# Differential attention: the joining factor moves to GpSimd, reciprocals go ahead of a maximum, row sums of squares go to ScalarE

## What is computed

```
def block(args):
    qb, start = args
    q_chunk = (start + jnp.arange(Q_BLOCK)) // CHUNK
    mask = key_chunk[None, :] <= q_chunk[:, None]
    s = jnp.einsum('bqhcd,bkhcd->bhcqk', qb, k).astype(jnp.float32)
    p = jax.nn.softmax(jnp.where(mask, s, -jnp.inf), axis=-1)
    a = p[:, :, 0] - lam * p[:, :, 1]
    return jnp.einsum('bhqk,bkhe->bqhe', a.astype(v.dtype), v)
...
o = rms_norm_2(o, subln_g) * (1.0 - lam_init)
return o.reshape(B, S, H * DIFF_V_DIM) @ w_out
```

## Time and profile before

| what | value |
|---|---|
| median of three runs | 2334.5 us |
| the profiled execution | 2334.52 us |
| its span | 2332.8 us |
| TensorE busy | 2311.1 us, 99% of the span |
| VectorE busy | 791.1 us, 34% |
| ScalarE busy | 853.1 us, 37% |
| GpSimd busy | 1173.1 us, 50% |
| PE busy from 1231 to 1322 us (the 32 tiles) | 82.63 us of 91 |
| granted TensorE clock | 1.00 |

### The profile page before, as it was taken

The page is one execution under the profiler, slowest core; times in us unless marked ns, Lnnn a source line. Parts: engine busy times, 40 slices in busy tenths (PEclk is TensorE's granted clock), DMA queues, the critical chain, the costliest instruction groups (busy, mean ns, idle before and its releaser), DMA issues.

```text
span 2332.8 us, 26900 instructions
## 1 busy us (share of the span) xinstructions
PE 2311.1 (99%) x11100; PEld 1882.2 (81%) x11100; DVE 791.1 (34%) x1372; ACT 853.1 (37%) x1258; POOL 1173.1 (50%) x978
## 2 busy tenths in 40 slices
PE   9999999999999999999999999999999999999999
PEld 7888888888977888888887688888887757888887
DVE  3222204864223222201467652022046954210310
ACT  4322214514343332222446543123156464421330
POOL 6544445636654544444552365444446944544442
PEclk9999999999999999999999999999999999999999
DMA  4323223212332232322220133233231202323322
GB/s 153 106 90 99 99 90 111 91 56 90 127 109 73 93 106 90 100 99 90 91 91 19 55 93 106 90 96 103 90 96 63 91 1 73 91 93 106 91 90 90
DMA packets 147584, 209.61 MB, mean 90 GB/s; under 512 B 7259, under 2 KB 113926, under 8 KB 147462
## 3 DMA queue, kind: packets, MB, share of 16 engines
q1 hardware_dynamic: 147462, 207.89, 27.6%
HBM read 205.77 MB, written 2.10 MB: 89 GB/s over the span
## 4 chain that ended last, share of the span: by engine, by line
PE 91%; DVE 4%; POOL 3%; issue 1%; ACT 1%; DMA 0%; SPq 0%; DVEq 0%; POOLq 0%; ACTq 0%
PE ps L1547 28%; PE ps L1548 28%; PE ps L1549 28%; POOL wlo L801 1%; DVE small L2967 1%; PE ps L2385 1%; PE ps L1919 1%; PE ps L1941 1%; PE ps L2310 0%; PE ps L2356 0%; PE ps L2366 0%; PE ps L2026 0%; DMA xrows<-in_x 0%; DVE small L2975 0%; DVE d_a L2980 0%
## 5 line engine op out<-in xcount | busy, mean ns | idle before, releaser
L801 POOL TENSOR_TENSOR wlo<-raw,whi 128x512 fp32r<-128x512 f32 x772 | 1006.1, 1336 | 973.2 <-ACT whi L1026 951.3
L1026 ACT ACTIVATE whi<-raw 128x2048 fp32r<-128x2048 f32 x184 | 350.6, 1905 | 632.5 <-DMA raw<-in_mlp_w 302.1
L1547 PE MATMUL ps<-hh,whi 128*128 128x512 f32 x1432 | 561.6, 392 | 0.0
L1549 PE MATMUL ps<-hh,wlo 128*128 128x512 f32 x1432 | 557.4, 389 | 0.0
L1548 PE MATMUL ps<-hl,whi 128*128 128x512 f32 x1432 | 557.3, 389 | 0.0
L1547 PEld LDWEIGHTS ps<-hh,whi 128*128 128x128 f32 x1432 | 268.8, 188 | 58.2 <-issue 2.3
L1549 PEld LDWEIGHTS ps<-hh,wlo 128*128 128x128 f32 x1432 | 268.8, 188 | 56.2
L1548 PEld LDWEIGHTS ps<-hl,whi 128*128 128x128 f32 x1432 | 268.9, 188 | 56.0 <-issue 1.2
L1547 PE MATMUL ps<-gh,whi 128*128 128x512 f32 x736 | 286.3, 389 | 0.0
L1548 PE MATMUL ps<-gl,whi 128*128 128x512 f32 x736 | 286.3, 389 | 0.0
L1549 PE MATMUL ps<-gh,wlo 128*128 128x512 f32 x736 | 286.3, 389 | 0.0
(11 more groups left out here) (472 smaller groups left out, 2869.4 us busy)
## 6 DMA issues: line engine op xcount, KB each, us to landing
raw<-in_mlp_w SPq DMA_DIRECT2D x64, 1024.0 KB, 5.4
raw<-in_ffn_w_up SPq DMA_DIRECT2D x22, 1024.0 KB, 5.2
raw<-in_ffn_w_down SPq DMA_DIRECT2D x22, 1024.0 KB, 4.8
raw<-in_ffn_w_gate SPq DMA_DIRECT2D x21, 1024.0 KB, 5.1
raw<-in_w_in SPq DMA_DIRECT2D x12, 1024.0 KB, 5.2
raw<-in_diff_w_in SPq DMA_DIRECT2D x12, 1024.0 KB, 5.0
raw<-in_xattn_w_kv SPq DMA_DIRECT2D x8, 1024.0 KB, 5.0
raw<-in_dsa_w_in SPq DMA_DIRECT2D x8, 1024.0 KB, 4.9
```

The source lines that it names most:

```text
L801: nc.gpsimd.tensor_tensor(wlo[i][:, c], raw[i][:, c], whi[i][:, c].bitcast(F32), ALU.subtract).then_inc(s_lo, 1)
L1026: nc.scalar.activation(whi[i][:, 0:width(made[0])], raw[i][:, 0:width(made[0])], ACT.Copy)\
L1547: nc.tensor.matmul(dst, w_hi, x_hi, start=start, stop=False)
L1549: return nc.tensor.matmul(dst, w_lo, x_hi, start=False, stop=stop)
```

## The change

1. VectorE's `weights` is cut in two. `inverse_sums(u)` takes the reciprocals; for qt = 0 it also makes the joining factor, as before, now in another cell. For qt = 1 to 3 the factor is made on GpSimd by `weight_factor(u)` from the same numbers. `weights(u)` waits for it and makes `d_a`.
2. The order on VectorE changes. At qt = 1 and 2 the reciprocals of tile u+1 go ahead of `max_(u+2)`, at qt = 0 and 3 behind it. `weights(u+1)` is always the last of the step, so behind `max_(u+2)` and, at qt = 0, behind `low` and `rows_copy`.
3. `row_sums` is gone. ScalarE squares each head in four instructions of 128x128 that also give the row sums, in place of one of 128x512, and GpSimd makes the half variance (`head_variance`).
4. On GpSimd the order is now by tile. Block b+12 is split a quarter at a time in steps 6 to 9, block b+13 in steps 28 to 31, and block b+14 behind the last head.
5. Two semaphores are merged into one with other counts, with no change of order.

```
+            def split_piece(q):
+                b = cut[0]
+                i = b % NBUF
+                if q == 0:
+                    pool.wait_ge(s_hi, b)
+                nc.gpsimd.tensor_tensor(wlo[i][:, ts(q, 512)], raw[i][:, ts(q, 512)],
+                                        whi[i][:, ts(q, 512)].bitcast(F32), ALU.subtract).then_inc(s_lo, 1)
+                if q == 3:
+                    cut[0] += 1
...
             def diff(b):
                 split_to(b + DIFF_BLOCKS - 1)
-                for h in range(8):
-                    head_scaled(h)
-                    if h in (0, 5, 6):
-                        split_to(b + DIFF_BLOCKS + (0, 5, 6).index(h))
+                for u in range(32):
+                    h, qt = divmod(u, 4)
+                    if qt:
+                        weight_factor(u)
+                    if qt == 2 and h:
+                        head_variance(h - 1)
+                    if qt == 3 and h:
+                        head_scaled(h - 1)
+                    if 6 <= u < 10 or 28 <= u:
+                        split_piece(u % 4 if u >= 28 else u - 6)
+                head_variance(7)
+                head_scaled(7)
+                split_to(b + DIFF_BLOCKS + 2)
+
+            def weight_factor(u):
+                h, qt = divmod(u, 4)
+                k, r = 12 + 2 * slot(u), 32 + 8 * (h % 2) + 2 * qt
+                n = 3 * h + qt
+                pool.wait_ge(s_drec, n)
+                if n > 1:
+                    pool.wait_ge(s_da, u if qt > 1 else u - 1)
+                nc.gpsimd.tensor_scalar(small[:, 8:9], small[:, k:k + 1], small[:, r + 1:r + 2], lam[:, 2:3],
+                                        ALU.mult, ALU.mult).then_inc(s_dfac, 1)
+
+            def head_variance(h):
+                pool.wait_ge(s_dosq, h + 1)
+                nc.gpsimd.tensor_scalar(newton[:, 0, 0:4], small[:, 24:28], -0.5 / P, -0.5 * EPS, ALU.mult, ALU.add)\
+                    .then_inc(s_dovar, 1)
...
                     act.wait_ge(s_dor, h + 1)
                     if h:
-                        act.wait_ge(s_doss, h)
-                    nc.scalar.activation(d_osq[:, :], d_o[:, h % 2, :], ACT.Square).then_inc(s_dosq, 1)
+                        act.wait_ge(s_dovar, h)
+                    for st in range(ST):
+                        r = nc.scalar.activation(d_osq[:, ts(st, P)], d_o[:, h % 2, ts(st, P)], ACT.Square,
+                                                 accum_out=small[:, 24 + st:25 + st])
+                    r.then_inc(s_dosq, 1)
...
                 for u in range(32):
                     h, qt = divmod(u, 4)
-                    if qt == 2:
-                        weights(u + 1)
+                    if qt in (1, 2):
+                        inverse_sums(u + 1)
                     if u < 30:
                         max_(u + 2)
-                    if qt != 2 and u < 31:
-                        weights(u + 1)
+                    if qt in (0, 3) and u < 31:
+                        inverse_sums(u + 1)
                     if qt == 0 and h >= 2:
                         low(h - 2)
                     if qt == 0 and h:
                         rows_copy(h - 1)
-                    if qt == 1 and h:
-                        row_sums(h - 1)
+                    if u < 31:
+                        weights(u + 1)
```

More of the change, by code:

```diff
@@ L456, in two_blocks @@
         s_fsq = sem("s_fsq")
-        s_frow = sem("s_frow")
+        s_drec = sem("s_drec")
+        s_dfac = sem("s_dfac")
         s_fcopy = sem("s_fcopy")
@@ L463, in two_blocks @@
         s_dosq = sem("s_dosq")
-        s_doss = sem("s_doss")
         s_dors = sem("s_dors")
@@ L2084, in diff @@
                                                     ident[:, :])
-                        r.then_inc(s_frow, 1)
+                        r.then_inc(s_fsq, 1)
                     half_group(b + 2 * g + 1, 4 * g, 1, (0, 1))
@@ L2263, in dsa @@
                         if j == 1 and a == 1:
-                            pe.wait_ge(s_fsq, 9)
+                            pe.wait_ge(s_fsq, 10)
                             pe.wait_ge(s_x, x0 + 8)
@@ L2950, in diff @@
                     if g == 0:
-                        dve.wait_ge(s_frow, 1)
+                        dve.wait_ge(s_fsq, 6)
                         V.tensor_copy(rstd[:, :], ps[:, 6, :]).then_inc(s_fcopy, 1)
@@ L2967, in max_, with inverse_sums @@
                     V.tensor_reduce(small[:, k:k + 2], two, AX_X, ALU.min).then_inc(s_dmax, 1)
-                def weights(u):
+                def inverse_sums(u):
                     h, qt = divmod(u, 4)
@@ L2973, in weights @@
                     k, r = 12 + 2 * slot(u), 32 + 8 * (h % 2) + 2 * qt
-                    dv.link(V.reciprocal(small[:, r:r + 2], small[:, k:k + 2]))
-                    dv.link(V.tensor_scalar(small[:, 8:9], small[:, k:k + 1], small[:, r + 1:r + 2],
+                    rec = V.reciprocal(small[:, r:r + 2], small[:, k:k + 2])
+                    if qt:
+                        rec.then_inc(s_drec, 1)
+                        return
+                    dv.link(rec)
+                    dv.link(V.tensor_scalar(small[:, 9:10], small[:, k:k + 1], small[:, r + 1:r + 2],
                                             lam[:, 2:3], ALU.mult, ALU.mult))
+                def weights(u):
+                    h, qt = divmod(u, 4)
+                    if qt:
+                        dve.wait_ge(s_dfac, 3 * h + qt)
                     if u >= 3:
@@ L2979, in weights @@
                     nk = P * (qt + 1)
-                    V.scalar_tensor_tensor(out=d_a[:, u % 3, 0:nk], in0=d_p[:, u % 3, 1, 0:nk], scalar=small[:, 8:9],
-                                           in1=d_p[:, u % 3, 0, 0:nk], op0=ALU.mult, op1=ALU.add).then_inc(s_da, 1)
+                    f = 8 if qt else 9
+                    V.scalar_tensor_tensor(out=d_a[:, u % 3, 0:nk], in0=d_p[:, u % 3, 1, 0:nk],
+                                           scalar=small[:, f:f + 1], in1=d_p[:, u % 3, 0, 0:nk],
+                                           op0=ALU.mult, op1=ALU.add).then_inc(s_da, 1)
                 def rows_copy(h):
@@ L2991, in rows_copy @@
                         .then_inc(s_dor, 1)
[L2993 to L3000, removed]
                 def low(h):
@@ L3009, in diff @@
                 max_(1)
+                inverse_sums(0)
                 weights(0)
@@ L3029, in diff @@
                 rows_copy(7)
-                row_sums(7)
                 low(6)
@@ L3043, in dsa @@
                     if t > 5:
-                        dve.wait_ge(s_fsq, t)
+                        dve.wait_ge(s_fsq, t + 1)
                     first = c_esq[:, 0, :] if t == 5 else sq[:, 1, :]
@@ L3047, in dsa @@
                 dve.wait_ge(s_eacc, acc_at(E_DSA) + 3)
-                dve.wait_ge(s_fsq, 8)
+                dve.wait_ge(s_fsq, 9)
                 V.tensor_tensor(sq[:, 0, :], sq[:, 0, :], sq[:, 1, :], ALU.add).then_inc(s_fsq, 1)
```

## The result

The changed kernel takes 2345.31 us in the median of 6 runs (2343.99 to 2346.16), the kernel before 2335.61 us in the same set (6 runs, 2334.26 to 2337.02). The ratio is 1.0042, with an interval of 1.0032 to 1.0052. I had forecast 2340.9 us with a range of 2336.5 to 2343: slower is right, but the time lies above the range. The profiled executions are 2334.52 and 2343.99 us, with spans of 2332.8 and 2341.8, so 9.0 us have to be found in the trace. (The other 0.5 us between these two times lies outside the spans.)

The account below looks back on a forecast made before the run. PE was taken to bound the kernel, with 91% of the chain of waits. To 2334.5 us the forecast added 2.0 for the 32 tiles and 4.4 for the late split: 2340.9 us, range 2336.5 to 2343.

Parts of the forecast that it names:

- The late split: GpSimd splits block b+14 only behind head 7's scaling, so PE stands before that block: +4.4 us, range 4.2 to 5.1.
- The lock-out rule: VectorE with two SBUF inputs and GpSimd reading SBUF exclude each other for a whole instruction; b+14 stall then 4.7 us.
- Nothing later gives it back: Behind PE's wait for block b+14, later work follows PE's own progress, so the 4.4 us delay is not recovered.
- The quarters of blocks b+12 and b+13 come earlier than `use` needs them: On GpSimd, the splits of these two blocks are early enough for their user; no time was added for them.
- The squares: Four ScalarE squares of 1.44 us delay the exponents of qt = 3: +0.35 us a head in heads 2 to 5.
- the sign of being right: Period of a middle head of 11.3 to 11.5 us, named in advance as showing the forecast right.
- Heads 6 and 7: Head 6 was given +0.3 us, an estimate by the same loop; head 7, with no maximum following, 0.
- rival B: The heads gain and lose nothing and only the late split is seen: 2338.9 us, chance 20%.
- Rival A: VectorE's relief reaches PE, whose idle 8.4 us in the 32 tiles could all go: 2330.5 us, chance 6%.
- Rival D: Each tile pays for making the factor on GpSimd, up to 1.26 us per factor: 2347.3 us, chance 5%.
- the sign that I had named for it: VectorE idle waiting for GpSimd's factor, named in advance as showing Rival D.
- Rival C: The late split is hidden by something unseen and only the heads count: 2336.5 us, chance 7%.

Follow-up runs that it names:

- experiment 1: The changed kernel with the split of block b+14 moved ahead of head 7's variance and scaling on GpSimd; 2337.83 us, ratio 1.0013 to the kernel before.
- experiment 5: The kernel before with one edit: the split of block b+14 behind head 7's scaling instead of ahead of it; 2342.17 us, ratio 1.0030.
- Experiment 4: The changed kernel with 19 unneeded matmuls on PE ahead of its wait for block b+14; 2343.46 us, ratio 1.0037 to the kernel before.
- Experiment 2: The changed kernel with the quarters of block b+12 split in steps 7 to 10 instead of 6 to 9; 2342.61 us, ratio 1.0036 to the kernel before.
- experiment 6: Experiment 3 with one 128x512 square on ScalarE, row sums and half variance back on VectorE; 2332.97 us, ratio 0.9991 to the kernel before.
- experiment 7: Experiment 6 with the joining factors back on VectorE, straight ahead of `d_a`; 2335.88 us, ratio 1.0003 to the kernel before.
- experiment 3: The changed kernel with both moves, b+14's split ahead of head 7's scaling and b+12's quarters one step later; 2335.95 us, ratio 1.0005 to the kernel before.
- experiment 8: Experiment 3 with the joining factors back on VectorE, straight ahead of `d_a`; 2336.55 us, ratio 1.0008 to the kernel before.

## Why the prediction was right, and where it failed

*The late split: right.* +4.4 forecast, +4.46 measured; experiment 1 takes it out, experiment 5 makes it alone. The split took 5.38 us, between the undisturbed 5.04 and the 6.00 beside VectorE: its start at 1338.34 overlaps the last `final_scaled`, which ends at 1338.92. Only its first quarter is slow, 1.72 us where the others take 1.25, and it ends at 1340.06. The lock-out rule of the Trainium skill (SBUF — State Buffer, Who interferes with whom), which the prediction put beside its sum, would have it wait for the end of `final_scaled` and end at 1340.17 (1338.92 + 1.25). So the trace agrees with it to 0.1 us here, and an undisturbed split is ruled out.

*What comes behind the wait: missing.* The sum had no term for the clock. "Nothing later gives it back" was true, but something later was added: 1.73 us behind this wait. Experiment 4 shows that PE's idleness is the cause. Its size could not be read from the kernel before, where the longest wait of this stage, 1.0 us, left the clock at 1.00. The Trainium skill (TensorE: Matmul & The Clock Gate, Loop structure matters more than you think) warns of a loop in which a long DMA wait stands ahead of each matmul, so that the matmul runs cold. Here the wait is for a split on GpSimd, and the 4.30 us of it, with a clock of 0.54 behind, agree. I had worked out the wait of 4.4 us and did not ask what PE does after it.

*"The quarters of blocks b+12 and b+13 come earlier than `use` needs them": the step that failed.* The sentence is correct and answers the wrong question. I checked who needs the quarters. I did not check what stands behind a quarter on GpSimd: since the change, a factor for which `d_a` and then PE wait. The quarter of step 6 waits for ScalarE's rounding, so the factor waits with it, 1.38 us on VectorE and 2.27 on PE, and the clock again adds 1.2. Experiment 2 brings 2.6 of the 2.9 us back; the 0.3 that stay are the forecast for this head. For the split of b+14 I had asked just this question; it had to be asked for every instruction that the change put into the same queue.

*The squares: right in kind, too large.* +0.35 a head forecast, +0.1 measured in heads 2 to 5, and the period is 11.2 where I had named 11.3 to 11.5 as the sign of being right. The term that was mis-sized is 4 x 0.36; the distance from one square to the next is 0.295 us (1.18 / 4), near the low end of 0.28. With 1.18 in place of 1.44 us the same sum gives +0.09 a head, so the formula holds there. Heads 6 and 7, for which it gave +0.3, gain 0.35 together; the reason stays open. For the heads, then, this was nearly rival B.

*Rival A* (the relief reaches PE) fails in the changed kernel but is half right: experiment 6 against 7 shows that moving the factors does reach PE, 0.33 us a head, once the squares no longer hold up the exponents and no quarter the factor. *Rival D* (a costly factor) is refuted in its cause: the factor takes 0.34 us, under the maximum. But the sign that I had named for it did appear, VectorE idle for GpSimd's factor, and it came from the quarters. In the whole stage there are three such waits, 2.4 us together: 1.4 at tile 7, and 0.5 each at tiles 29 and 31. Each time a quarter of a split stands straight ahead of the factor. Those of block b+13 at tiles 29 and 31 are still there in experiment 3. The groups up to 1320 us, so without tile 31:

```profile
L959 POOL TENSOR_SCALAR small<-small,lam 128x1 f32<-128x1 f32 x23 | 7.8, 341 | 39.9 <-DVE small L3014 39.9
L3031 DVE SCALAR_TENSOR_TENSOR d_a<-d_p,small 128x512 f32<-128x512 f32 x7 | 5.2, 745 | 1.4 <-POOL small L959 1.4
```

*Rival C* fell with PE's wait of 4.30 us.

Altogether: a forecast of 6.4 us consisted of 4.4 right and 2.0 of which 0.4 came. The 9.0 us of the trace are 4.46 of split, 1.4 of factor 7, 2.9 of slow clock behind the two, and 0.4 for the rest of the heads, less 0.15 behind the stage. The direction was right for the reason given, the late split. The time went out of the range by the two terms that the sum did not have, 4.3 us together.

## What to carry to other kernels

When an engine with slack is given a small instruction on the critical path, go through its whole queue: for each instruction ahead of the small one ask what it waits for, not when its own result is due. A wait on TensorE that is longer than any the kernel had before can have a second price, the slow clock behind it, here 1.2 us for a wait of 2.3 and 1.7 to 2.5 for one of 4.3. And price the parts of a change apart: here the factors on GpSimd gained, the row sums on ScalarE lost about as much, and two places in an order hid both.

## What the runs showed of the hardware

The clock behind a standstill of PE: waits of up to 1.36 us (experiment 8) left it at 1.00 in this stage. Behind 2.3 us it fell to 0.50, which is 1.2 GHz, in all three traces with such a wait (the changed kernel, experiments 1 and 4), and cost 1.2 us until it was back. Behind 4.3 us with nothing in its place it fell in all three traces as well, and cost 1.7 us in the changed kernel, 1.8 in experiment 5 and 2.5 in experiment 2. Behind 1.8 us ahead of the last tile it fell in two traces (experiments 2 and 4, for 1.35 and 1.6 us) and stayed at 1.00 in three (the changed kernel, experiments 1 and 3); behind the 1.95 us of experiment 7 it also stayed:

```profile
1316.22 0.44 PE L2149 MATMUL ps<-ident,d_a 128*128 128x128 f32 x2 [1.95 <-DVE d_a L3026]
...
1316.00:1320.00 4.00, 3.04 (x17) 2.25 (x17) 3.80 (x11) 3.19 (x9) 0.00 (x0) 1.00 0.00 0
```

What decides between these I could not find. It may be part of why executions of one of these kernels lie 2 to 4 us apart. The mean clocks fit that without showing it: in experiment 6, whose longest wait in this stage is 1.25 us, all 11 executions have 1.000, in experiment 7 eight of ten have 0.999, and in experiment 1 the one with 1.000 is also the shortest, 2335.63 us, 1.9 under the next.

A square of 128x128 with its row sum, followed by the accumulator's read of 0.19 us, keeps ScalarE for 0.295 us; one of 128x512 without sums lasts 0.62, so the four sums cost 0.56 us there, where VectorE's reduction takes 0.68 in time that it had free.

The ports: `d_a` of qt = 0 takes 709 ns in the mean of the changed kernel, now that the scaling of `head_scaled` runs beside it. The same instruction before:

```profile
1266.66 0.35 DVE L2980 SCALAR_TENSOR_TENSOR d_a<-d_p,small 128x128 f32<-128x128 f32 x1
```

And after, VectorE, then GpSimd:

```profile
1280.42 0.87 DVE L3031 SCALAR_TENSOR_TENSOR d_a<-d_p,small 128x128 f32<-128x128 f32 x1
1280.11 1.04 POOL L981 TENSOR_TENSOR d_o<-d_o,small 128x512 f32<-128x512 f32 x1
```

It ends at 1281.29, behind GpSimd's end at 1281.15. The Trainium skill (SBUF — State Buffer, Who interferes with whom) says that a VectorE instruction with two SBUF inputs contends with a GpSimd instruction that reads SBUF, and that the port pair they share is an exclusive lock. The trace agrees in kind, 0.87 for 0.35 us; if the lock held for the whole of GpSimd's instruction, `d_a` would have had to run its 0.35 us after 1281.15, and it ends 0.21 us sooner than that. For the quarter of the split beside `final_scaled`, above, the same reckoning is 0.11 us too long. PE's scores, 0.92 us from 1280.41, just cover it here.
